# Moving matmul tiles by 64 bytes, and folding the second attention's forget sums and low value parts into its other products

## The reference

```
def _forgetting_attention(q, k, v, cum_log_f):
    """softmax_s( q_t.k_s/sqrt(d) + F[t] - F[s] ), s <= t, F = cumsum log f."""
...
        z = jnp.einsum('bhtd,bhsd->bhts', qb, kb).astype(jnp.float32) * scale
        z = z + cum_log_f[:, :, start:end, None] - cum_log_f[:, :, None, :end]
...
        z = jnp.where(s_idx <= t_idx, z, NEG_BIG)
        p = jax.nn.softmax(z, axis=-1)
        outs.append(jnp.einsum('bhts,bhsd->bhtd', p.astype(vb.dtype), vb))
```

## Time and profile before

| | |
|---|---|
| median of 3 runs | 1290.13 us (1289.41 to 1290.8) |
| the profiled execution | span of 1286.8 us from the first to the last instruction; its whole time isn't given |
| instructions | 17060 |
| PE, matmuls | busy 1254.0 us (97%), 6226 of them |
| PE, weight loads | busy 1044.0 us (81%) |
| DVE | 758.9 us (59%) |
| ACT | 586.3 us (46%) |
| POOL | 748.3 us (58%) |

### The profile page before, as it was taken

One profiled execution on the slowest core, in us unless ns is written; L12 is line 12 of the kernel. 1 busy time (PEld: TensorE's weight loads), 2 busy tenths in 40 slices (PEclk: granted clock), 3 DMA queues, 4 the chain that ended last, 5 costly groups with the idle time before them and its releaser, 6 DMA issues.

```text
span 1286.8 us, 17060 instructions
## 1 busy us (share of the span) xinstructions
PE 1254.0 (97%) x6226; PEld 1044.0 (81%) x6226; DVE 758.9 (59%) x1245; ACT 586.3 (46%) x956; POOL 748.3 (58%) x863
## 2 busy tenths in 40 slices
PE   5999999999999999999999999999999999999997
PEld 4777878878888888887778988887888888888887
DVE  5868778334444367698787337754367616651565
ACT  3375667445664446233456644434333313331332
POOL 2644443434333676676545878535659957885782
PEclk9999999999999999999999999999999999999999
DMA  9412223222344733233224444212323333333322
GB/s 381 173 66 79 93 82 140 86 95 99 107 130 135 242 120 99 82 99 103 68 68 158 138 148 131 81 52 66 98 65 99 112 102 98 98 99 99 90 90 66
DMA packets 43107, 142.74 MB, mean 111 GB/s; under 512 B 4880, under 2 KB 7440, under 8 KB 41872
## 3 DMA queue, kind: packets, MB, share of 16 engines
q1 hardware_dynamic: 42768, 141.39, 33.6%
q10 hardware_dynamic: 256, 0.26, 0.1%
HBM read 130.88 MB, written 8.39 MB: 108 GB/s over the span
## 4 chain that ended last, share of the span: by engine, by line
PE 79%; DVE 14%; ACT 4%; issue 1%; POOL 1%; DMA 1%; SPq 0%; DVEq 0%; ACTq 0%; POOLq 0%
PE ps L124 78%; DVE tm L134 2%; DVE tm L137 2%; ACT tm L131 2%; ACT L131 1%; DVE ac L137 1%; PE ps L128 1%; DVE spl L134 1%; DVE tm L142 1%; DVE sph L145 1%; DVE x L137 1%; DVE ewl L134 1%; DMA x<-xin 1%; DVE ma L137 1%; POOL ycl L134 0%
## 5 line engine op out<-in xcount | busy, mean ns | idle before, releaser
L134 POOL TENSOR_TENSOR wl<-raw,wh 128x256 fp32r<-128x256 f32 x804 | 691.3, 892 | 480.6 <-ACT wh L131 472.7
L131 ACT ACTIVATE wh<-raw 128x1024 fp32r<-128x1024 f32 x201 | 212.0, 1055 | 310.8 <-PE ps L124 304.9
L124 PE MATMUL ps<-hh,wh 128*128 128x512 f32 x872 | 344.4, 395 | 0.0
L124 PE MATMUL ps<-hh,wl 128*128 128x512 f32 x872 | 340.2, 390 | 0.0
L124 PE MATMUL ps<-hl,wh 128*128 128x512 f32 x872 | 339.9, 390 | 0.0
L124 PEld LDWEIGHTS ps<-hh,wl 128*128 128x128 f32 x872 | 163.9, 188 | 34.9
L124 PEld LDWEIGHTS ps<-hh,wh 128*128 128x128 f32 x872 | 164.2, 188 | 33.3 <-DVE tm L137 0.4
L124 PEld LDWEIGHTS ps<-hl,wh 128*128 128x128 f32 x872 | 164.2, 188 | 32.9
L134 DVE TENSOR_TENSOR tm<-tm,tm 128x512 f32<-128x512 f32 (+4 forms) x113 | 94.3, 839 | 42.1 <-ACT tm L131 38.9
L137 DVE SCALAR_TENSOR_TENSOR tm<-cb,par_sb,tm 128x512 f32<-128x512 f32 x88 | 87.1, 990 | 50.5 <-ACT tm L131 47.1
L131 ACT ACTIVATE tm<-tm 128x512 f32<-128x512 f32 (+3 forms) x109 | 54.0, 531 | 80.5 <-DVE tm L137 64.5
(11 more groups left out here) (308 smaller groups left out, 2273.5 us busy)
## 6 DMA issues: line engine op xcount, KB each, us to landing
raw<-units SPq DMA_DIRECT2D x201, 512.0 KB, 3.5
ada<-units SPq DMA_DIRECT2D x16, 512.0 KB, 14.5
kept<-ge SPq DMA_DIRECT2D x16, 256.0 KB, 2.5
tm<-kept SPq DMA_DIRECT2D x16, 256.0 KB, 3.5
tm<-gate_w SPq DMA_DIRECT2D x12, 256.0 KB, 4.0
x<-xin SPq DMA_DIRECT2D x2, 1024.0 KB, 6.1
x<-xin SPq DMA_DIRECT2D x1, 2048.0 KB, 9.5
out<-x SPq DMA_DIRECT2D x16, 128.0 KB, 1.8
```

The lines of the kernel that those rows point to most:

```text
L124: return self.none if self.e is None else self.e.matmul(out, lhs, rhs, start=start, stop=stop, skip_group_check=skip)
L131: return self.none if self.e is None else self.e.activation(out, in_, func, **kw)
L134: return self.none if self.e is None else self.e.tensor_tensor(out, a, b, op)
```

## The change

First, tiles move by 64 bytes. A constant `HALF_LINE` = 64 is added ahead of `MTh`, `MTl` and everything behind them, and `stat` shrinks from 64 to 32 columns. Counted modulo 128 bytes, `MTh` and `MTl` then start at 64, while `ZH`, `ZL`, `Oh`, `Ol`, `YAh`, `VAh`, `VBh`, `MG2h`, `YDh`, `YCh`, their low parts, and `Q2`, `K2`, `PTh`, `V2h` start at 0, like the weights. Further additions ahead of and behind `ATh`/`ATl` and `CKh`/`CKl` leave those four at 64. The 512 byte steps within the tiles keep these remainders.

Second, the forget sums lose their own matmul. Two new tiles `KF` hold, for each half, the head's high keys on its own 64 rows, and on the other 64 rows the forget sums (high part in 8 rows, low part in 8 rows, the rest zero). The matmul with the queries' low part now moves `KF` instead of `K2`, and the rows of `QL0` that were zero get a one-hot column pattern from the constants. That costs new DVE work: for each head a copy into `QL0` and a copy into `KF`, and two more small copies at the start.

Third, the low value parts lose their own matmul. A tile `VB` has, for each head, 64 high columns beside 64 low columns, and one matmul with `PTh` and one with `PTl` make both; the upper 64 rows of the result hold the low part's share. ACT copies those to a tile `FO` (`low_half`, behind `gate(h + 8)` in its list), and DVE adds them (`gate_y`). The product of low values and low probabilities is computed too.

```
@@ qk_b, PE @@
+            pe.wait_ge(s_kf, c, x)
+            pe.wait_ge(s_hot, c, x)
...
-                pe.mm(PS[b][:, 0:n], QL0[p][x][:, w], K2[p][x][:, 0:n], False, False)
-                pe.mm(PS[b][:, 0:n], conr[0:72, CO + h:CO + h + 1].to_broadcast([72, 128]), FT[0:72, 0:n], False, False)
+                pe.mm(PS[b][:, 0:n], QL0[p][x][:, w], KF[x][:, 0:n], False, False)
@@ pv_b, PE @@
-                vh, vl = (x[:, j, c * 128:(c + 1) * 128] for x in (VBh, VBl))
+                both = VB[:, j, 128 * h:128 * h + 128]
                 pe.wait_ge(s_vl, "b", j)
-                pe.mm(PS[b][:, 128 * j:T], vh, PTh[:, j, 128 * j:T], j == 0, False)
-                pe.mm(PS[b][:, 128 * j:T], vh, PTl[:, j, 128 * j:T], False, False)
-                last = pe.mm(PS[b][:, 128 * j:T], vl, PTh[:, j, 128 * j:T], False, j == 3)
+                pe.mm(PS[b][:, 128 * j:T], both, PTh[:, j, 128 * j:T], j == 0, False)
+                last = pe.mm(PS[b][:, 128 * j:T], both, PTl[:, j, 128 * j:T], False, j == 3)
@@ scalar_program @@
+        def low_half(h):
+            if h:
+                act.wait_ge(s_fold, h - 1)
+            act.wait_ge(s_pv, "b", h)
+            act.fn(FO[:, :], PS[6 + h % 2][64:128, :], ACT.Copy).then_inc(*s_half_out.up(h))
...
             gate(h + 8)
+            low_half(h)
@@ vector_program @@
+        def key_copy(c, x):
+            own = HALVES[x][0]
+            dve.wait_ge(s_kh, "b", c, x)
+            if c:
+                dve.wait_ge(s_z, "b", 2 * c - 1, 0)
+            dve.cp(KF[x][own, :], K2[c % 2][x][own, :]).then_inc(*s_kf.up(c, x))
...
+                    if br == "b":
+                        h = 2 * c + x
+                        dve.cp(QL0[p][x][other, :],
+                               conr[other, CO + h:CO + h + 1].to_broadcast([64, T])).then_inc(*s_hot.up(c, x))
...
+                    if br == "b" and c:
+                        key_copy(c, x)
@@ gate_y @@
             dve.wait_ge(s_pv, br, h)
+            if br == "b":
+                dve.wait_ge(s_half_out, h)
+                o = PS[6 + h % 2]
+                dve.tt(o[r:r + 64, :], o[0:64, :], FO[:, :], ALU.add).then_inc(*s_fold.up(h))
+                dve.wait_ge(s_fold, h)
@@ forget sums, vector_program @@
-        dve.cp(FT[0:8, :], f1).then_inc(*s_fd.up("fh"))
+        dve.cp(KF[1][0:8, :], f1).then_inc(*s_fd.up("fh"))
+        dve.cp(KF[0][64:72, :], f1).then_inc(*s_fd.up("fh0"))
...
-        dve.cp(FT[64:72, :], f0).then_inc(*s_fd.up("ft"))
+        dve.cp(KF[1][32:40, :], f0).then_inc(*s_fd.up("fl1"))
+        dve.cp(KF[0][96:104, :], f0).then_inc(*s_fd.up("ft"))
+        for x in range(2):
+            key_copy(0, x)
@@ pool_program @@
-        pool.zero(f32(FT[:, :])).then_inc(*s_fz.up(0))
...
+            if name == ("f", 0):
+                pool.wait_ge(s_pv, "a", 7)
+                for x in range(2):
+                    last = pool.zero(f32(KF[x][:, :]))
+                last.then_inc(*s_fz.up("keys"))
```

More of the change, by code:

```diff
@@ L24 @@
 U = 1024
+HALF_LINE = 64
 PARAMS = [("norm_g", 8), ("b_ada", 24), ("b_gate", 16), ("norm_mix_g_2", 8), ("norm_cross_g_2", 8),
@@ L68, in constants @@
         out[h, o + h] = 1.0
-        out[64 + h, o + h] = 1.0
+        for r in (32, 64, 96):
+            out[r + h, o + h] = 1.0
     inv = np.power(np.float32(500000.0), -(np.arange(0, 16, 2, dtype=np.float32) / np.float32(16)))
@@ L267, in build @@
     KVT = at("kvt", [P, KC, T], F32, h0)
-    MTh = at("mth", [P, KC, M], F32R, h0 + 16384)
-    MTl = at("mtl", [P, KC, M], F32R, h0 + 24576)
+    off[0] += HALF_LINE
+    MTh = at("mth", [P, KC, M], F32R, h0 + 16384 + HALF_LINE)
+    MTl = at("mtl", [P, KC, M], F32R, h0 + 24576 + HALF_LINE)
     TM = [at(f"tm{i}", [P, T], F32) for i in range(7)]
@@ L275, in build @@
     sm = at("sm", [P, 96], F32)
-    stat = at("stat", [P, 64], F32)
+    stat = at("stat", [P, 32], F32)
     nrm = at("nrm", [P, 96], F32)
@@ L295, in build @@
     VAl = at("val", [P, 4, T], F32R)
+    KF = [at(f"kf{x}", [P, T], F32R, a1 + 4096 + 8192 * x + 6144) for x in range(2)]
     vb0 = off[0]
+    VB = at("vb", [P, 4, 2 * T], F32R, vb0)
     VBh = at("vbh", [P, 4, T], F32R)
@@ L321, in build @@
     SZ = [at(f"sz{i}", [P, T], F32) for i in range(2)]
-    FT = at("ft", [P, T], F32R)
+    FO = at("fo", [64, T], F32)
     MA = at("ma", [P, U], F32, a1)
@@ L423, in build @@
     s_fz, s_fd, s_fa, s_fp = sig("s_fz"), sig("s_fd"), sig("s_fa"), sig("s_fp")
+    s_hot, s_kf, s_half_out, s_fold = sig("s_hot"), sig("s_kf"), sig("s_half_out"), sig("s_fold")
     s_bias, s_pe, s_rc, s_pn, s_dn = sig("s_bias"), sig("s_pe"), sig("s_rc"), sig("s_pn"), sig("s_dn")
@@ L468, in build, with heads, per_head @@
     eps = con_raw[:, 9:10]
+    def heads(tile, t, part):
+        return tile[:, t, :].rearrange("p (h x d) -> p h x d", h=8, x=2)[:, :, part, :]
+    def per_head(bank):
+        return bank[:, :].rearrange("p (h d) -> p h d", h=8)
     def mg(tiles, k):
@@ L779, in pv_b @@
         def pv_b(h):
-            c, b = h // 2, 6 + h % 2
+            b = 6 + h % 2
             take(b)
@@ L1413, in vproj @@
                         if br == "b":
-                            act.wait_ge(l_mout[t // 2], 0)
+                            act.wait_ge(l_mout[0], 0)
+                            act.wait_ge(l_mout[1], 0)
                         if t != v_rows(br)[3]:
@@ L1422, in vproj @@
                                    scale=sm[:, 64 + t:65 + t]).then_inc(*s_vh.up(br, t))
+                        elif br == "b":
+                            act.fn(heads(VB, t, 0), per_head(PS[2 + t]), ACT.Copy).then_inc(*s_vh.up(br, t))
                         else:
@@ L1521, in scalar_program @@
         act.fn(TM[0][0:8, :], TM[0][0:8, :], ACT.Ln, bias=1.0).then_inc(*s_fa.up("ln"))
-        vproj("b", "bv", VBh)
+        vproj("b", "bv", None)
         def qk_b(h):
@@ L2031, in v_low @@
                             ALU.subtract).then_inc(*s_vl.up(br, t))
+                elif br == "b":
+                    split_low(heads(VB, t, 1), per_head(PS[2 + t]), heads(VB, t, 0), (br, t), s_vl)
                 else:
                     split_low(dl[:, t, :], PS[2 + t][:, :], dh[:, t, :], (br, t), s_vl)
+        def key_copy(c, x):
[4 more added lines that the diff above has]
+            dve.cp(KF[x][own, :], K2[c % 2][x][own, :]).then_inc(*s_kf.up(c, x))
         def qk_low(br, c, step, heads=(0, 1)):
@@ L2185, in gate_add @@
                     dve.stt(o, t[:, :], pcol("c", k), o, ALU.mult, ALU.add).then_inc(*s_mod.up(*key))
-        v_low("b", VBh, VBl)
+        v_low("b", None, None)
         qk_b(0)
```

4 lines of the change are left out of this document (2 added, 2 removed).

## The result

The changed kernel takes 1301.76 us, the median of six runs (1297.13 to 1303.01), against 1289.81 us of the kernel before beside it: a ratio of 1.0084 with a 95% interval of 1.0072 to 1.0095. It is 0.8% slower, where 0.4% faster was forecast. The profiled execution has a span of 1295.3 us and is the fastest of the six, at 1297.13 us, with a mean granted clock of 0.988 where the six together have 0.985, so its rows show rather less of the low clock than the median run has.

A forecast was written before the change was run, and what follows sets the result against it. PE was taken as the bound, busy nearly throughout the second attention. Span 1286.8 - 5.3 (move) - 10.3 (fewer matmuls) + 8.9 (waits) + 1.7 (clock) = 1281.8; the runs' median lies 3.3 above: 1285.1 us, range 1281.5 to 1289.5.

The forecast's parts named there:

- The clock: Second attention, near 400 us: PE's waits bring one fall to half clock, +1.7 us; none or two falls as ends.
- The slower rival: At `qk_b(7)` the low clock goes on, doubling 14 us of PE work: 1294.6 us, chance 0.08.
- The waits: PE waits added ahead of `qk_b(3)`, `qk_b(5)`, `qk_b(7)`, `pv_b(7)`, `mod_end`: 0.6, 0.6, 3.3, 2.8, 0.9 us.
- The chain up to the fold: Head 6: ACT starts its gate at 393.20, the half copy follows, DVE's fold starts at 395.36 us.
- Head 0: `qk_b(0)`: small and key copies ahead of DVE's subtractions delay the last bank, so its 0.66 us is not gained, +0.7.
- Fewer matmuls: Second attention: dropped forget and value-low matmuls save 0.66 and 0.63 us a head, together -10.3 us for eight heads.
- The move: Tiles moved by 64 bytes: long rows -2.9, short rows -3.3, last output blocks +0.9, together -5.3 us.
- so the distance counts and not the place: 256 column matmuls: distance modulo 128 sets the step, 119 ns at equal remainders, 113 ns when 64 apart.
- The first rival: The distance of two tiles costs nothing and the row differences belong to the stages: 1290.4 us, chance 0.09.
- the range: Whole kernel: the measured time lies between 1281.5 and 1289.5 us, chance 0.77 to 0.8.
- Faster: Whole kernel: faster than before by more than about 0.2%, that is under 1287.5 us, chance 0.75.
- The rival without waits: Second attention: no wait takes the place, `low_half` is ready earlier or the turn is covered: 1275.2 us, chance 0.07.

The follow-up runs named there:

- e5: Changed kernel plus 12 useless matmuls behind each gate half ahead of `qk_b(7)` and `pv_b(7)`: 1293.54 us, 1.0025 of the kernel before.
- e9: Changed kernel with every tile at the address of before, so without the 64 byte move: 1297.86 us, 1.0069 of the kernel before.
- e12: The program of e9 run again beside the changed kernel on one chip: 1299.74 us, 1.0075 of the kernel before.
- e1: Kernel before with only the tiles moved by 64 bytes, second attention as before: 1289.53 us, 1.0009 of the kernel before.
- e3: Changed kernel with `low_half(h)` moved ahead of the silu and `gate(h+8)` on ACT: 1278.26 us, 0.9918 of the kernel before.
- e8: Kernel of e3 with every tile at the address of before, so without the move: 1281.33 us, 0.9941 of the kernel before.
- e4: Separate test running only matmuls at varied distances of moving from stationary tile; at 512 columns 227 ns at 0, 229 at 64, 233 at 192 bytes.
- e10: e3 with `ATh`/`ATl` and `CKh`/`CKl` put at 192 bytes and `gate_add(6)` behind `turn_b(7)` on DVE: 1277.77 us, 0.9919 of the kernel before.

## Why the prediction was wrong

The mechanism was right, in place and in order; two terms of the sum were too small, and the larger of them decided the sign.

**The clock is the step that failed.** The prediction put it so: "I count one such fall, +1.7; none and two are the ends." Over the runs the changed kernel loses 19.0 us to the clock and the kernel before 6.0, so the term is 13.0, and even the upper end was 3.4. In the profile there are 17.1 us at half clock instead of 3.4: one low stretch behind `qk_b(7)`, two together at `pv_b(7)`, one behind `mod_end`, and one far behind, at the norm. I had weighed each wait by itself against the one fall seen near 103 us, and had not counted the wait of `mod_end` as a place at all. e5 shows that it is the idleness: with PE kept busy in two of the places, some 9 of the 13.0 are gone. But not all of the 13.0 belongs to the waits. Without the move (e9, e12) the same waits come with 14.2 us lost, 8.2 more than before; the other 4.8 came with the move, as 4.0 did in e1, and why is not shown. So the waits' clock is 8 to 9 us against the 1.7 forecast, and the rest is a loss that the prediction had at nothing. The slower rival named this cause and the right place, but as one long stretch from `qk_b(7)`; what came were several short ones with full clock between them, and its 1294.6 was too low as well.

**The waits** were forecast at 0.6, 0.6, 3.3, 2.8 and 0.9, 8.2 us, as additions to before, and came at 1.2, 1.2, 3.9, 3.3 and 1.6, some 11.3. Each is 0.5 to 0.7 too short. The chain up to the fold was right: from the gate copy to the fold lie 388.59 to 390.95, 2.36 us, against 393.20 to 395.36 and with them 2.2 in the prediction. Behind it the durations were taken from the earlier trace rows, and the low part `val` took 1.09 us and not 0.69; for even heads the second sum took 1.21 and not 0.74. The reason is below.

**Head 0**: counted from the start of the matmul ahead of it, `qk_b(0)` took 2.36 us to the next group's first matmul (276.78 to 279.14) where before it took 2.51 (276.08 to 278.59). So 0.15 of its 0.66 was gained, and the term is +0.5 where +0.7 was forecast.

**Fewer matmuls**: 0.66 + 0.63 = 1.29 us a head were forecast. In e3 the first matmuls of `qk_b(2)` and `qk_b(6)` lie 302.51 to 373.58 apart, 71.07 us for four heads against 76.19 before, 1.28 a head, which is right.

**The move** was put at -5.3 and is 3.5 to 3.9 in the products of e1 and of e9 against the changed kernel, 1.8 in that of e8 against e3, where few runs stand behind it. In time e1 gained nothing clear of noise (1.0009, 0.9997 to 1.0022), since the clock took it back. Long rows came as forecast, 687 to 680. The step that failed is "so the distance counts and not the place" together with modulo 128: the short rows that took 113 ns had 64 bytes, like `mth` and `ckh` after the change, but in the changed kernel the groups with `mth` moving and those of `ckh` take 353 ns, and only those with `mth` stationary, 192 apart, take 340. By e4 that fits a distance with its sign. The rows that misled, those of `zh` before, fit no such rule: they had 64 bytes too and took 113 ns, and 118 in e12. So `MTh`/`MTl` gain 64 groups by 20 and 64 by 7, 1.7 us and not 2.4; `CKh` and `ATh` 0.3 and not 0.9. The first rival, by which the distance costs nothing, is refuted by e4: the step goes from 227 to 233 ns with nothing but the address of one operand changed. The Trainium skill's page SBUF — State Buffer (Who interferes with whom) has PE read its two operands through independent ports and wait on nobody. As the prediction read that rule, e4 speaks against it; what PE waits for there is not shown.

**The sum with the measured terms**, against the mean of before: 1289.8 - 10.3 - 3.9 + 11.3 + 0.5 + 13.0 = 1300.4, where 1300.3 was measured. The -3.9 and the 13.0 come out of the clock of these same runs, so the agreement tests only the other terms. Without the clock's term it would be 1287.4, inside the range.

"Faster" had 0.75 because all but one rival took the clock for a detail. The rival without waits is e3: it was put at 1275.2, and 1278.26 was measured.

## What to carry to other kernels

Where PE is fed without a gap, price a new wait twice: once as itself, and once for the clock that may fall behind it; here 11.3 us of new waits brought another 8 to 9 us of lost clock. Then look at the order of the lists before the cost of the work: the same fold and the same copies cost 23.5 us more or less depending on one line's place behind an instruction that waits for PE's last unit. If a wait can't be removed, work that nobody needs can be the cheaper filling, and a comparison of two versions should look at time times clock beside the time.

## What was not expected of the hardware

The distance of moving and stationary tile changes the step of a matmul, and long and short rows want different distances. A distance of 0 gave 227 to 228 ns at 512 columns in e4 and in `hh` against `wh` of every kernel, and 120 at 256. At 64 or 192 bytes there are two values: 229 or 233 at 64 and 512 columns (e9 and e12), and 113 or 118 at 256 columns (e4, e10, e12), each with one and the same pair of addresses. At 128 columns the distance made no difference (e4). So a layout can be priced from the first kind and not safely from the second.

DVE took longer for operations on SBUF alone while POOL was at work. Two key copies of one form in the changed kernel, with what follows them on DVE, and POOL's row beside the second:

```profile
376.06 0.42 DVE L147 CAST kf<-k 64x512 fp32r<-64x512 f32 x1
...
377.24 0.93 DVE L147 CAST kf<-k 64x512 fp32r<-64x512 f32 x1
378.20 0.69 DVE L150 TENSOR_REDUCE stat<-ps 128x1 f32<-128x512 f32 x1
...
377.15 2.30 POOL L136 TENSOR_TENSOR wl<-raw,wh 128x256 fp32r<-128x256 f32 x3 [3.97 <-ACT wh L133]
```

The second copy takes twice the first, and the maximum behind it, which reads PSUM, its usual 0.69. The other two late pairs of key copies show the same (0.42, then 0.91 to 0.93). `val` takes 1.10 in all four odd heads of the changed kernel, each time with POOL at work for half of it, and 0.69 in all four before, without POOL. In e3 it is 0.69 again: there DVE reads its operands before ACT's copy of the next weight unit, which starts POOL, and the second sum behind it takes 1.23 instead, in three of the four heads, where nothing waits for it. So the place behind the gate also moved DVE's work into POOL's time, 0.4 us of each wait. By the Trainium skill's page SBUF — State Buffer (Who interferes with whom), DVE and POOL share a pair of ports that one instruction locks to its end, and DVE needs it for operations with two SBUF inputs or in a two-port mode. The rows agree.
